# Feed-forward up projections as seven half-tile products, in two chunks, on one Trainium2 core

## The reference

```python
def swiglu(x, w_in, w_out):                 # w_in 1024 x 5632, w_out 2816 x 1024
    gate, up = jnp.split(x @ w_in, 2, axis=-1)
    return (jax.nn.silu(gate) * up) @ w_out

# first block
x = x + 0.5 * swiglu(rmsnorm(x, n1_g), ffn1_w_in, ffn1_w_out)
h = rmsnorm(x, n2_g); ...                   # projections, two attention branches, gates
x = x + merged @ w_out
x = x + 0.5 * swiglu(rmsnorm(x, n3_g), ffn2_w_in, ffn2_w_out)
x = rmsnorm(x, nf_g)
# second block
x = x + 0.5 * swiglu(rms_norm(x, n1), wi1, wo1)
x = x + stick_breaking_attention(rms_norm(x, mix_norm), ...)
x = x + 0.5 * swiglu(rms_norm(x, n2), wi2, wo2)
```

## Time and profile before

| | |
|---|---|
| median of 3 runs | 2073.12 us |
| the profiled execution, first to last instruction | 2072.0 us |
| TensorE busy | 2065.4 us (100%), 9514 matmuls |
| its weight loads (PEld, beside the matmuls) | 1680.8 us (81%) |
| VectorE, ScalarE, GpSimd busy | 781.5, 775.8, 853.3 us (38, 37, 41%) |
| TensorE clock granted | full in all slices |

### The profile page before, as it was taken

One profiled execution on the slowest core, in us unless ns is written; L12 is line 12 of the kernel. 1 busy time (PEld: TensorE's weight loads), 2 busy tenths in 40 slices (PEclk: granted clock), 3 DMA queues, 4 the chain that ended last, 5 costly groups with the idle time before them and its releaser, 6 DMA issues. The chain is left out here.

```text
span 2072.0 us, 26411 instructions
## 1 busy us (share of the span) xinstructions
PE 2065.4 (100%) x9514; PEld 1680.8 (81%) x9514; DVE 781.5 (38%) x1286; ACT 775.8 (37%) x1056; POOL 853.3 (41%) x360
## 2 busy tenths in 40 slices
PE   9999999999999999999999999999999999999999
PEld 7888888777778888888888888888878878888887
DVE  5222211667763432222116222211588863222200
ACT  5322222344443433322323333222677754222221
POOL 2444545333332444444544444454422344444543
PEclk9999999999999999999999999999999999999999
DMA  5223333422121332223332322333344432222332
GB/s 187 90 93 101 102 102 109 138 82 72 62 72 62 102 102 92 91 100 101 99 115 91 101 91 91 102 112 101 109 134 130 131 98 88 99 101 100 103 107 76
DMA packets 64383, 209.11 MB, mean 101 GB/s; under 512 B 7936, under 2 KB 8960, under 8 KB 64320
## 3 DMA queue, kind: packets, MB, share of 16 engines
q1 hardware_dynamic: 62912, 205.49, 30.8%
q10 hardware_dynamic: 1408, 2.78, 0.4%
HBM read 193.69 MB, written 2.10 MB: 94 GB/s over the span
## 5 line engine op out<-in xcount | busy, mean ns | idle before, releaser
L439 POOL TENSOR_TENSOR w_lo<-raw,w_hi 128x1024 fp32r<-128x1024 f32 x356 | 853.1, 2410 | 1200.2 <-ACT w_hi L971 1058.9
L479 PE MATMUL ps<-xn_hi,w_hi 128*128 128x512 f32 x1896 | 744.2, 393 | 0.1
L481 PE MATMUL ps<-xn_hi,w_lo 128*128 128x512 f32 x1896 | 738.3, 389 | 0.0
L480 PE MATMUL ps<-xn_lo,w_hi 128*128 128x512 f32 x1896 | 738.0, 389 | 0.0
L971 ACT ACTIVATE w_hi<-raw 128x1024 fp32r<-128x1024 f32 (+1 forms) x362 | 366.8, 1044 | 166.2 <-PE ps L481 154.9
L479 PEld LDWEIGHTS ps<-xn_hi,w_hi 128*128 128x128 f32 x1896 | 356.0, 188 | 77.2 <-issue 4.8
L481 PEld LDWEIGHTS ps<-xn_hi,w_lo 128*128 128x128 f32 x1896 | 355.9, 188 | 74.8
L480 PEld LDWEIGHTS ps<-xn_lo,w_hi 128*128 128x128 f32 x1896 | 356.1, 188 | 72.3 <-issue 0.2
L1313 DVE TENSOR_TENSOR scratch<-ps,rstd 128x512 f32<-128x512 f32 x200 | 137.7, 690 | 573.9 <-PE ps L481 569.4
L479 PE MATMUL ps<-h_hi,w_hi 128*128 128x512 f32 x704 | 273.9, 389 | 0.0
L480 PE MATMUL ps<-h_lo,w_hi 128*128 128x512 f32 x704 | 273.9, 389 | 0.0
(11 more groups left out here) (208 smaller groups left out, 1426.9 us busy)
## 6 DMA issues: line engine op xcount, KB each, us to landing
raw<-weights SPq DMA_DIRECT2D x358, 512.0 KB, 3.4
k_hi_twice<-sb_k_hi SPq DMA_DIRECT2D x31, 128.0 KB, 2.3
k_lo_twice<-sb_k_lo SPq DMA_DIRECT2D x31, 128.0 KB, 2.3
x_sb<-x_t SPq DMA_DIRECT2D x8, 256.0 KB, 6.0
bias<-rel ACTq DMA_DIRECT2D x1, 2048.0 KB, 11.1
q_both<-sb_q_hi SPq DMA_DIRECT2D x16, 128.0 KB, 2.2
q_both<-sb_q_lo SPq DMA_DIRECT2D x16, 128.0 KB, 2.3
out_t<-x_sb SPq DMA_DIRECT2D x7, 256.0 KB, 4.5
```

The costliest lines, as they stand in the source:

```text
L439: nc.gpsimd.tensor_tensor(w_lo[s][:, :, :], raw[s][:, :, :], w_hi[s][:, :, :].bitcast(F32), ALU.subtract).then_inc(S["lo_done"], 1)
L479: pe.matmul(to, w_hi[s][:, k, :], hi, start=opens, stop=False)
L480: pe.matmul(to, w_hi[s][:, k, :], lo, start=False, stop=False)
L481: last = pe.matmul(to, w_lo[s][:, k, :], hi, start=False, stop=ends)
```

## The change

A pair of gate and up tiles is a 2 x 2 product: the weights split into two halves of four pieces along the input channels (gate and up, first and second half), the input into the same channel halves and two halves of 256 tokens. Instead of eight block products the kernel forms seven (P1 to P7, a form of Strassen's algorithm), each 4 pieces x 3 matmuls of 256 columns. Three of the seven take a plain quarter of the weights (quads 1, 2 and 4); four take sums that VectorE makes of raw weights (`sum_1` to `sum_4`, into `s1` to `s4`). Each is rounded by ScalarE as a half unit; GpSimd makes the remainder of six, VectorE that of the seventh (`rest_of_7`). On the input side four products take T tiles (t1 to t4), differences of input tiles that are made once per feed-forward, behind the residual updates before it, and split into hi and lo. VectorE adds the products up out of PSUM, 256 tokens at a time, through three banks of each parity.

The 22 tiles are cut into chunks of 12 and 10, each followed by its part of the down projection over 8 output tiles (2 units each, of 8 and 4 or 4 and 6 pieces), so that `x_sb` is updated twice. The first unit of a chunk's down projection stands between P7 and P4 of the chunk's last tile. The first four tiles of the first feed-forward stay in the plain form. Hardware loops are gone: every instruction is written out. The attention stages keep their order.

```diff
-DOWN = [(0, 8), (8, 16), (16, FT)]
...
+QUAD = UK // 2
+HALVES = [slice(0, TOK // 2), slice(TOK // 2, TOK)]
+CUT = 12
+CHUNKS = [(0, CUT), (CUT, FT)]
+DOWN_PARTS = [[(0, 8), (8, CUT)], [(CUT, 16), (16, FT)]]
+DOWN_ORDER = [(0, 0), (1, 0), (0, 1), (1, 1)] + [(k, e) for k in range(2, DT) for e in range(2)]
+PLAIN = 4
...
+PLACE = {1: (0, 0), 5: (0, 1), 6: (1, 0), 2: (1, 1), 7: (2, 0), 4: (3, 0), 3: (3, 1)}
...
+        def rest_7(n, F, i):
+            pool.wait_ge(S["q_hi"], HI_COUNT[n, F, i])
+            nc.gpsimd.tensor_tensor(quad_of(n, i, w_lo), factor(n, F, i, raw, s_sum),
+                                    quad_of(n, i, w_hi).bitcast(F32), ALU.subtract).then_inc(S["q_lo"], 1)
+        def ffn(n):
+            for c, (_, end) in enumerate(CHUNKS):
+                first = seven_from(n, c)
+                for i in (1, 5, 6):
+                    rest_7(n, first, i)
+                for F in range(first, end):
+                    more = F + 1 < end
+                    rest_7(n, F, 2)
+                    if more:
+                        rest_7(n, F + 1, 1)
+                    else:
+                        rest_down(n, c, 0)
+                    rest_7(n, F, 4)
+                    if more:
+                        rest_7(n, F + 1, 5)
+                    rest_7(n, F, 3)
+                    if more:
+                        rest_7(n, F + 1, 6)
+                for at in range(1, DOWN_TURNS):
+                    rest_down(n, c, at)
...
+        def product(n, F, i, part=(0, QUAD)):
+            b, p = banks_of(n, F), PAIR[n, F]
+            if part[0] == 0:
+                if i == 7:
+                    pe.wait_ge(S["lo7_done"], p + 1)
+                else:
+                    pe.wait_ge(S["q_lo"], LO_COUNT[n, F, i])
+            half = HALVES[0] if i in (1, 2) else HALVES[1]
+            to = PS[:, b[{1: 0, 2: 0, 6: 1, 7: 1, 4: 1, 5: 2, 3: 2}[i]], 0:TOK // 2]
+            w = quad_of(n, i, w_hi), quad_of(n, i, w_lo)
+            for k in range(*part):
+                if i in T_OF:
+                    hi, lo = t_hi[:, k, T_OF[i], :], t_lo[:, k, T_OF[i], :]
+                else:
+                    hi, lo = (x[:, k if i == 1 else QUAD + k, half] for x in (xn_hi, xn_lo))
+                opens = i in (1, 5, 6) and k == 0
+                pe.matmul(to, w[0][:, k, :], hi, start=opens, stop=False, skip_group_check=True)
+                pe.matmul(to, w[0][:, k, :], lo, start=False, stop=False, skip_group_check=True)
+                last = pe.matmul(to, w[1][:, k, :], hi, start=False, stop=(k == QUAD - 1), skip_group_check=True)
+            if part[1] == QUAD:
+                last.then_inc(S[f"p{i}_done"], 1)
...
+                        if F >= first + 2:
+                            pe.wait_ge(S["g1_made"], p - 1)
...
+                    product(n, F, 1)
+                    if F >= first + 2:
+                        pe.wait_ge(S["c12_made"], p - 1)
+                    product(n, F, 5)
+                    if F > first:
+                        pe.wait_ge(S["v2_made"], p)
+                        product(n, F - 1, 4)
+                    if F >= first + 2:
+                        pe.wait_ge(S["c21_made"], p - 1)
+                    if F == first and c == 0:
+                        pe.wait_ge(S["t_lo"], QUAD)
+                    product(n, F, 6)
+                    if F > first:
+                        pe.wait_ge(S["c22_made"], p)
+                        product(n, F - 1, 3)
+                    pe.wait_ge(S["p1_copied"], p + 1)
+                    product(n, F, 2)
+                pe.wait_ge(S["v1_made"], p + 1)
+                product(n, F, 7)
...
+            p = PAIR[n, end - 1]
+            down(n, c, 0)
+            pe.wait_ge(S["v2_made"], p + 1)
+            product(n, end - 1, 4)
+            pe.wait_ge(S["c22_made"], p + 1)
+            product(n, end - 1, 3)
...
+        def round_7(n, F, i):
+            u, p = up_unit(n, F, 0), PAIR[n, F]
+            if i in (1, 2):
+                landed(u)
+            elif i == 4:
+                landed(u + 1)
+            else:
+                act.wait_ge(S[{5: "s1_made", 6: "s2_made", 7: "s3_made", 3: "s4_made"}[i]], p + 1)
+            if F == seven_from(n, int(F >= CUT)):
+                act.wait_ge(S["unit_done"], DONE[u - NSLOT + PLACE[i][0] + 1])
+            else:
+                act.wait_ge(S[f"p{i}_done"], p)
+            copy(quad_of(n, i, w_hi), factor(n, F, i, raw, s_sum)).then_inc(S["q_hi"], 1)
...
+            for F in range(first, end):
+                more = F + 1 < end
+                if not (opening and F == first):
+                    copy_p1(n, F)
+                    if F > first:
+                        round_7(n, F, 2)
+                    round_7(n, F, 7)
+                    if more:
+                        round_7(n, F + 1, 1)
+                    else:
+                        round_down(n, c, 0)
+                round_7(n, F, 4)
+                if more:
+                    round_7(n, F + 1, 5)
+                round_7(n, F, 3)
+                if more:
+                    round_7(n, F + 1, 6)
+                else:
+                    round_down(n, c, 1)
+                if F > first:
+                    silu(n, F - 1)
+                    round_h(n, F - 1)
...
+        def sum_4(n, F):
+            gate = raw[up_unit(n, F, 0) % NSLOT]
+            dve.wait_ge(S["s2_made"], PAIR[n, F] + 1)
+            weights_read(n, F, 3)
+            nc.vector.tensor_tensor(s_sum[3][:, :, :], gate[:, QUAD:UK, :], s_sum[1][:, :, :], ALU.subtract)\
+                .then_inc(S["s4_made"], 1)
...
+        def rest_of_7(n, F):
+            dve.wait_ge(S["q_hi"], HI_COUNT[n, F, 7])
+            nc.vector.tensor_tensor(quad_of(n, 7, w_lo), s_sum[2][:, :, :], quad_of(n, 7, w_hi).bitcast(F32),
+                                    ALU.subtract).then_inc(S["lo7_done"], 1)
+        def add_p6(n, F):
+            b, beta, p = F % 2, banks_of(n, F)[1], PAIR[n, F]
+            dve.wait_ge(S["p1_copied"], p + 1)
+            dve.wait_ge(S["p6_done"], p + 1)
+            dve.wait_ge(S["h_made"], FT * n + F - 1)
+            nc.vector.tensor_tensor(gate_of[b][:, second_half], PS[:, beta, first_half], up_of[b][:, first_half],
+                                    ALU.add).then_inc(S["v1_made"], 1)
...
+        def cycle(n, c, F):
+            first, end = seven_from(n, c), CHUNKS[c][1]
+            more, late = F + 1 < end, F > first
+            sum_4(n, F)
+            rest_of_7(n, F)
+            if late:
+                add_p4(n, F - 1)
+            if more:
+                sum_1(n, F + 1)
+            add_p6(n, F)
+            if more:
+                sum_2(n, F + 1)
+            if late:
+                add_p3(n, F - 1)
+                scale_gate_up(n, F - 1)
+            scale_gate_first(n, F)
+            if more:
+                sum_3(n, F + 1)
+            if n == 2 and 1 <= F <= DT:
+                k = F - 1
+                scale_two(X[:, k, :], X[:, k, :], gains[:, G_FINAL, k:k + 1], scratch[:, 6, :])\
+                    .then_inc(S["x_normed"], 1)
+            if late:
+                make_h(n, F - 1)
+            add_p7_p5(n, F)
+            if late:
+                split_h(n, F - 1)
...
+        def make_t(m, j):
+            k, made = QUAD + j, 3 * (QUAD * m + j)
+            gain = gains[:, FFN_INPUT[m], k:k + 1]
+            t2, t3, t4 = (t_raw[:, j, e, :] for e in range(1, 4))
+            nc.vector.scalar_tensor_tensor(t3, X[:, k, second_half], gain, xg[:, j, second_half],
+                                           ALU.mult, ALU.subtract).then_inc(S["t_made"], 1)
+            dve.wait_ge(S["t_made"], made + 1)
+            nc.vector.tensor_tensor(t2, t3, xg[:, j, first_half], ALU.add).then_inc(S["t_made"], 1)
+            dve.wait_ge(S["t_made"], made + 2)
+            nc.vector.scalar_tensor_tensor(t4, X[:, k, first_half], gain, t2, ALU.mult, ALU.subtract)\
+                .then_inc(S["t_made"], 1)
+        def split_t(m, j):
+            dve.wait_ge(S["t_hi"], QUAD * m + j + 1)
+            nc.vector.tensor_tensor(t_lo[:, j, 1:4, :], t_raw[:, j, 1:4, :], t_hi[:, j, 1:4, :].bitcast(F32),
+                                    ALU.subtract).then_inc(S["t_lo"], 1)
```

822 lines of the change are left out of this document (571 added, 251 removed).

## The result

| | before | after |
|---|---|---|
| median | 2073.2 us | 2279.5 us (2275.8 to 2285.3 over 4 runs) |
| ratio | | 1.0997, 95% interval 1.0981 to 1.1012 |
| profiled execution | 2072.0 us | 2277.3 us |

The kernel became 10% slower. The forecast was 2180 us with a range of 2080 to 2260: the direction and the main mechanism (VectorE and GpSimd taking turns) are the forecast's, and the time is 20 us above its upper end.

A forecast was written before the change was run, and what follows sets the result against it. TensorE, busy 2065.4 of 2072.0 us, was taken to bound the kernel before, with VectorE leading after the change. 2072 + 74 + 8 + 18 + 5 + 6 = 2183, + 1.1, rounded to 2180 us; range 2080 to 2260.

The forecast's parts named there:

- Part 1: Steady tile on TensorE: 84 matmuls of 256 columns at 0.121 us, 10.2 us a tile, alone saving 60 us.
- Rival D: TensorE's products: 256-column matmuls cost 0.17 us, a tile 14.3 us, in all 2360 us; chance 0.04.
- Part 2: In each tile, VectorE's instructions with two SBUF inputs and GpSimd's exclude each other: at least 11.5 us shared.
- Part 3: Order inside a steady tile, laid out by hand over the engines: 12.4 us a tile, bounds 11.4 and 13.4.
- Part 4: Ends of the eight chunks: 6.5 us off each, so 990 against 916 us (+74); +8 behind the last P3.
- Part 5: Feed-forward openings: reciprocals and what goes with them 18 us, x_sb scalings 5 us, T tiles 6 us.
- B: Steady tile: the engines pack better or exclude less, TensorE stays the bound at 10.2 us, 2030 us; chance 0.12.
- C: Steady tile: the exclusion holds, with near-perfect packing, 2095 us; chance 0.11.

## Why the prediction was right and wrong, step by step

**Part 1, products: right.** 0.120 us between matmuls, as a row of the changed kernel's TensorE shows:

```profile
857.24 0.28 PE L744 MATMUL ps<-t_hi,w_hi 128*128 128x256 f32 x1
857.36 0.28 PE L745 MATMUL ps<-t_lo,w_hi 128*128 128x256 f32 x1
857.48 0.28 PE L746 MATMUL ps<-t_hi,w_lo 128*128 128x256 f32 x1
```

Rival D is out. That the 0.17 us of the earlier trace rows was a late load fits this and was not shown.

**Part 2, the exclusion: right, and shown** by the short GpSimd instructions (1.42 to 0.68 us with nothing changed on VectorE; 233 us). The turn of 1.13 us taken for GpSimd is 1.155 by an estimate from the 1.70 us between two of its starts with a VectorE turn of 0.55 between them. Its scope was read too narrowly (two inputs only), which did no harm here, since a tile of the change has no fast one-input instruction between SBUF tiles.

**Part 3, the cycle: the step that failed most.** It gave 12.4 us; it is 13.20, and 84 x 0.8 = 67 us of the 94 us by which the span (2277.3) exceeds the sum (2183). The layout put ScalarE's copy of P1 at 1.93 us, behind P1 alone. In the code it also waits for `h_lo_done` of two tiles back, which the layout itself had last in VectorE's cycle. So ScalarE starts late, and behind it GpSimd (3.68 us of pause) and `rest_of_7` (0.94 us). The run with ScalarE's order changed shows that taking this wait away gives 0.26 us of the 0.8. The other 0.5 us stays when VectorE has no pause at all in its cycle: by the rows it lies in how long VectorE's instructions wait for a whole turn of GpSimd, where the layout had packed them closer. That is read and not tried, and which instructions it belongs to was not separated. The part's upper bound of 13.4 us held the value.

**Part 4, ends of chunks: right in sum.** The four chunks of 10 take 125.0, 126.7, 126.2 and 125.4 us of TensorE's time by the trace (first product to last, without the unit of the down projection), in the mean 6.1 less than 13.2 x 10, where 6.5 was taken off: 3 us over 8 chunks. Behind the last P3 TensorE waited for 0.4 us in one chunk of the eight, and not for 8 us.

**Part 5, openings: the second step that failed.** Some 50 us by the trace against 29: 9.5, 21.5 and 18.6, what the second, third and fourth feed-forward's chunks of 12 take above 13.2 x 12 - 6.1, with the wait ahead of the last one's first product. The reciprocals and what goes with them, forecast 18, are 13: some 8 for the reciprocals, measured, and some 5 for the third stage's other instructions, since without reciprocals its first period was still 17.4 us beside 12.5 in the two others. The x scalings, forecast 5, measured 5.9. The T tiles, forecast 6, are then some 31 by difference. That last is VectorE's list of 4.6 us for each of the last x tiles, 6.7 where two GpSimd turns fall in, in front of products that TensorE could have begun. With 1.2 us a tile of it off VectorE 10.4 us went. I had compared that list with a unit's 5.4 or 6.8 us of TensorE, which holds only while TensorE still has units to do; behind the last one nothing covers it. Why the fourth opening costs twice the second's was only read from the trace (VectorE works from 1852.5 to 1878.6 us with pauses of 0.25 us) and not tried.

**A term put at nothing: the first feed-forward.** It keeps four plain tiles, and the forecast gave its opening no cost. There too VectorE makes T tiles first: TensorE waits 5.3 us for the scaling of a plain tile (the row of line 667 above) behind them, and 2.5 us more for GpSimd's first remainder ahead of the first product, and part of that stretch ran at 1.2 GHz. Some 10 us of the 94 are there. With 67 for the cycle, 3 for the chunks' ends, 8 not spent behind them and 21 in the openings, that makes 93. Attention took the same time as before, within 2 us.

**The range.** Its upper end was below the sum with the text's own bounds. 13.4 us a tile gave 2268 there, and the openings had no bound at all; with 13.4 and openings doubled it would have been 2297. The two terms have only part of their cause in common: in the run with GpSimd's instructions short, with the period at TensorE's 10.08 us, the three openings still cost some 32 us, counted in the same way.

**The rivals.** B is a real floor (2046 us measured, 2030 forecast) that the changed kernel comes near only when the exclusion is taken away, or when 3.5 VectorE turns leave the tile (2082.5 us, TensorE without a pause in the steady part). C's near-perfect packing (11.4 us a tile) was in no run that kept all of VectorE's turns; 11.18 us came with three of them gone.

## What to carry to other kernels

Where two engines take turns on a port, count the turns per period on each, and move operands to PSUM or the work to another stage before reordering: here 3.5 turns fewer of VectorE's 8.5, and the ring opened, gave 197 us, while the one reordering tried gave 22. An edit was worth about its turn while both engines were in line, and could not be priced by turns once one had a pause; the same move of one remainder gained 52 us in one version and lost 30 in the next.

When laying out a cycle by hand, write beside each item *every* semaphore that it waits for, those that guard a buffer's reuse too. Those are what closes a ring from the end of one cycle to the head of the next.

And let the range reach at least as far as the sum with each term's own bound.

## What the runs showed that I had not expected

- A VectorE instruction from SBUF to SBUF with one input (0.42 us for 512 elements alone) takes turns with GpSimd as one with two inputs does (1.18 us beside it).
- Taking a VectorE turn away can leave the row of its neighbour longer by what it had waited: removing 1.78 us shortened the period by 0.60, and moving 1.37 us to the other engine shortened it by 0.8 while that engine had pauses.
- The granted clock was 0.968 in the mean with a TensorE pause of up to 2.6 us in each tile, and 0.990 with 16 matmuls more in each tile and a pause of 1.0 us; the time was the same.
